# Seven half-block products in the last gated up stage, second homes for the weight sums, and other places for the conditioning turns

## The chip, the core and the metric

One core of a Trainium2 chip runs the whole program. The metric is device time in microseconds (us), as the median of several executions. Profiles come from one execution each.

## What is computed

Two transformer-like blocks for 256 tokens and 1024 features, in fp32. What bears on the change is the last feed-forward part, `conv_ffn` of the second block (there are two of them, one per layer), and the conditioning:

```python
def conv_ffn(h, w_up, conv_w, conv_b, w_down):
    up = h @ w_up                                   # 1024 -> 2 x 2816
    up = lax.conv_general_dilated(up, conv_w[:, None, :], window_strides=(1,), padding=[(CONV_W - 1, 0)],
        dimension_numbers=('NWC', 'WIO', 'NWC'), feature_group_count=2 * D_FF_2) + conv_b     # CONV_W = 3
    val, gate = jnp.split(up, 2, axis=-1)
    return (jax.nn.silu(gate) * val) @ w_down       # 2816 -> 1024

cond = jax.nn.silu(c)
for i in range(DEPTH):
    mod = cond @ ada_w[i] + ada_b[i]                # 1024 -> 6144, for one row
```

The first block has `swiglu` in that place: `(silu(g) * u) @ w_down` without the convolution.

## The kernel before, in words

Activations lie feature-major: a tile is 128 features by 256 tokens. The program is one fixed list of instructions per engine, and semaphores order the engines. `STAGES` names the stages; `up0`, `up1`, `up2`, `up3` are the four gated up products with 44 weight tiles each, that is 22 pairs (gate tile and value tile), and `down0` to `down3` follow them. Both `up0` and `up1` belong to `swiglu`, `up2` and `up3` to `conv_ffn`.

**The ring (SyncE).** All weights come through four ring slots of 512 KB (`ring`, L428). Slot s is reloaded once TensorE has used slot s-4 and, where VectorE reads it too, once the sums are made. One in-order queue issues them. In the same queue stand 96 conditioning loads (`ada_in`, L437), each right behind the slot that `ADA_SLOTS` names. A conditioning load waits on `ada_used` until its home was read by VectorE. There are four homes for the first `N_WIDE` loads and two from then on. While the queue waits for that, no ring slot behind it is issued.

**Conditioning turns (VectorE).** `ada(n)` does n multiply-accumulates over 1024 columns (L2000 for the first of a column of blocks, L2002 else). Where they stand in VectorE's list is written into each stage: `adas_with` in `residual`, `ADA_TWICE` in `up1` (those pairs take two turns), `k >= 4` in `od_xb`, and so on.

**Plain pairs.** `up` (L703) multiplies a weight tile of 1024 x 128 with the tokens: eight matmuls of 256 columns, sixteen records in the trace since each shows as two. `conv_ffn` on ScalarE (L1371) then makes the first tap with the bias for both tiles (L1380) and the SiLU of the gate tile (L1385). On VectorE (L2271) come two more taps per tile (L2291, L2294), and the gate product (L2299). After products 8 and 16 `sum_mids` makes three sums of middle tiles for the down stage (L1794 to L1797).

**Pairs as seven products.** `quick_pair` (L677) computes a pair from half blocks: four of the seven products use sums of weights (`sum_pair`, L2178, four instructions over 512 columns), four use sums of tokens (`sum_tokens`, once per stage). Every product is four matmuls of 128 columns, eight records. Three parts pass through ScalarE, which copies the running sum out of the bank four times (`keep_part`, L1367). VectorE puts them together in `combine_pair` (L2187, L2190). In `up0` all pairs from 2 on go this way. Products 3, 5 and 7 add to the bank that the copies read, so TensorE waits there for `parts_kept`:

```python
pe.wait_ge(pair_sums, 4 * q + 2)
pe.wait_ge(parts_kept, 4 * q + 1)
added_product(chain, s2, t2).then_inc(pair_steps, 1)
```

**Down stages.** `down` (L611) has the same seven-product scheme in chunks; `sum_weights` (L1784) makes four sums per chunk into four homes in `probs_t` and `pair`. Each sum of chunk n waits for TensorE's use of the same sum of chunk n-1 (`weight_sums_used`).

## Time and profile before

| | |
|---|---|
| median of 3 runs | 1678.43 us (1678.21 to 1679.16) |
| the profiled execution | 1679.56 us, its span 1677.8 us |
| mean granted TensorE clock | 0.996 of full speed |
| TensorE busy | 1633.3 us, 97% of the span |
| VectorE busy | 1003.7 us, 60% |
| ScalarE busy | 353.7 us, 21% |
| GpSimd busy | 73.2 us, 4% |
| chain that ended last | TensorE 88%, VectorE 8%, DMA 2% |
| HBM read | 286.68 MB, 171 GB/s over the span |

The chain that ended last is followed back from the last instruction, at each step to what released it. A row of the timeline tells start, duration, engine, line, operation and tiles, and in brackets how long the engine was idle before it and what ended that. "PEclk" is the clock granted to TensorE as a share of full speed. The stages around the change stand at these times of the span: `up0` 238 to 374 us, `od_xb` 443 to 478, `up1` 682 to 839, `up3` 1451 to 1602, `down3` 1602 to 1672.

### The profile page before, as it was taken

To read this page: it belongs to the slowest core of one execution; us is meant where nothing else is said; L and a number is where in the kernel's file an instruction comes from. 1 tells how busy PE (TensorE), PEld (TensorE's weight loads), DVE (VectorE), ACT (ScalarE), POOL (GpSimd) and SP (SyncE) were. 2 spreads that over 40 slices of the span, in tenths; PEclk is the share of its full clock that TensorE was granted. 3 is DMA by queue.
4 is the path that set the end of the run, shared out by engine and by line. 5 is a ranking of instruction groups with operands and counts; after the bars stand their busy time and mean duration, and the time that the engine had idled before them with its cause. 6 is when DMAs were issued, how large, how long until landed. Compare 5 with 4: busy or idle time off the path is not lost.

```text
span 1677.8 us, 27211 instructions
## 1 busy us (share of the span) xinstructions
PE 1633.3 (97%) x10888; PEld 1428.4 (85%) x10888; DVE 1003.7 (60%) x2086; ACT 353.7 (21%) x825; POOL 73.2 (4%) x86
## 2 busy tenths in 40 slices
PE   7999999999989999999999999999999999999998
PEld 6758889999978867788899786688889998888898
DVE  6554668888655334586767577556645683434455
ACT  3241212220151102100001322422213131222200
POOL 0000000000000000195000000000000000000000
PEclk9999999999999999999999999999999999999999
...
GB/s 226 141 145 193 179 217 251 245 223 227 189 161 157 193 319 138 237 238 275 213 169 170 90 118 109 76 149 153 150 139 164 176 3 113 140 152 153 154 169 189
DMA packets 79901, 289.50 MB, mean 173 GB/s; under 512 B 8992, under 2 KB 10016, under 8 KB 79264
## 3 DMA queue, kind: packets, MB, share of 16 engines
...
q8 instruction: 87, 1.43, 0.4%
q14 instruction: 38, 0.31, 0.1%
HBM read 286.68 MB, written 1.05 MB: 171 GB/s over the span
## 4 chain that ended last, share of the span: by engine, by line
PE 88%; DVE 8%; DMA 2%; issue 1%; ACT 1%; SPq 0%; DVEq 0%; ACTq 0%
PE acc L480 46%; PE acc L611 16%; PE acc L669 4%; PE acc L571 4%; PE acc L1134 3%; PE acc L535 2%; PE acc L556 1%; DVE big L2178 1%; DMA ring<-stream 1%; PE acc L490 1%; PE acc L1113 1%; PE score L1099 1%; PE acc L751 1%; DVE bT L2002 1%; PE score L775 1%
## 5 line engine op out<-in xcount | busy, mean ns | idle before, releaser
L480 PE MATMUL acc<-H,ring 128*128 128x256 f32 x2864 | 631.1, 381 | 12.3 <-DMA ring<-stream 8.3
L480 PEld LDWEIGHTS acc<-H,ring 128*128 128x128 f32 x2864 | 544.1, 191 | 95.0 <-DMA ring<-stream 9.7
L480 PE MATMUL acc<-big,ring 128*128 128x256 f32 x880 | 192.2, 379 | 0.9 <-PE acc L480 0.9
L480 PEld LDWEIGHTS acc<-big,ring 128*128 128x128 f32 x880 | 166.8, 190 | 24.8 <-issue 2.3
L2291 DVE SCALAR_TENSOR_TENSOR pair<-acc,cols,pair 128x255 f32<-128x255 f32 x84 | 40.5, 483 | 114.9 <-ACT pair L1380 110.7
L2002 DVE SCALAR_TENSOR_TENSOR bT<-bT,cond 128x1024 f32<-128x1024 f32 x64 | 83.3, 1302 | 39.5 <-DMA bT<-ada_in 34.1
L1784 DVE TENSOR_TENSOR probs_t<-ring 128x512 f32<-128x512 f32 (+1 forms) x96 | 62.1, 647 | 58.5 <-PE acc L611 52.7
L611 PE MATMUL acc<-FFN,ring 128*128 128x128 f32 x760 | 93.6, 275 | 0.0
L611 PEld LDWEIGHTS acc<-FFN,ring 128*128 128x128 f32 x760 | 89.1, 192 | 0.6 <-issue 0.4
L1380 ACT ACTIVATE pair<-acc,cols 128x256 f32<-128x256 f32 x84 | 47.1, 564 | 164.5 <-PE acc L480 164.5
L1212 ACT ACTIVATE SQ<-X 128x256 f32<-128x256 f32 x56 | 23.4, 417 | 181.3 <-DVE X L1760 107.4
L535 PE MATMUL acc<-FFN,ring 128*128 128x256 f32 (+1 forms) x224 | 52.6, 388 | 8.4 <-DMA ring<-stream 8.4
L571 PE MATMUL acc<-ring,big 128*128 128x512 f32 x128 | 56.2, 593 | 1.6 <-DVE big L2402 1.6
L669 PE MATMUL acc<-big 128*128 128x128 f32 x480 | 56.9, 275 | 0.0
L1134 PE MATMUL acc<-MEM,ring 128*128 128x256 f32 x256 | 56.3, 381 | 0.1
L535 PEld LDWEIGHTS acc<-FFN,ring 128*128 128x128 f32 x224 | 43.5, 195 | 14.7 <-issue 8.4
L669 PEld LDWEIGHTS acc<-big 128*128 128x128 f32 x480 | 55.2, 192 | 0.0
L1134 PEld LDWEIGHTS acc<-MEM,ring 128*128 128x128 f32 x256 | 48.3, 190 | 7.2 <-ACT MEM L1606 0.5
L1643 POOL TENSOR_SCALAR chunk_tab<-cols,small 128x64 f32<-128x64 f32 x32 | 19.4, 651 | 706.7 <-DVEq L2064 706.7
L571 PEld LDWEIGHTS acc<-ring,big 128*128 128x128 f32 x128 | 24.2, 190 | 29.6 <-issue 27.3
L611 PE MATMUL acc<-FFN,probs_t 128*128 128x128 f32 x352 | 47.1, 275 | 0.0
L1760 DVE TENSOR_TENSOR X<-acc,X 128x256 f32<-128x256 f32 x32 | 13.6, 425 | 53.9 <-PE acc L480 47.5
...
## 6 DMA issues: line engine op xcount, KB each, us to landing
ring<-stream SPq DMA_DIRECT2D x440, 512.0 KB, 3.6
bT<-ada_in SPq DMA_DIRECT2D x76, 512.0 KB, 5.0
big<-ada_in SPq DMA_DIRECT2D x20, 512.0 KB, 4.8
...
```

Of the source, the lines that this page charges most:

```text
L480: mm = nc.tensor.matmul(dst, w[:, k * cols_per:(k + 1) * cols_per], r, start=first and n == 0, stop=last and n == len(src) - 1)
L535: mm = nc.tensor.matmul(acc[t % 4][:, 0:width], w[:, k * P:(k + 1) * P], src(k, width), start=k == 0, stop=k == KD - 1)
L571: mm = nc.tensor.matmul(acc[(t + b) % 4][:, :], src[:, k * S + b * P:k * S + b * P + P], w[:, k % 2 * 512:(k % 2 + 1) * 512], start=k == 0 ...
L611: mm = nc.tensor.matmul(dst, w[:, k * P:(k + 1) * P], x[k], start=first and k == 0, stop=last and k == len(x) - 1)
L669: mm = nc.tensor.matmul(dst, w[:, k * P:(k + 1) * P], x[k], start=first and k == 0, stop=k == len(x) - 1, skip_group_check=True)
L1134: mm = nc.tensor.matmul(acc[(TILE0["glu"] + k) % 4][:, 0:S], w[:, i * P:(i + 1) * P], at(MEM, i), start=n == 0, stop=n == KD - 1)
L1212: nc.scalar.activation(at(SQ, k), at(src, k), ACT.Square).then_inc(norm_squares, 1)
L1380: nc.scalar.activation(at(pair, 2 * (k % 2) + e), at(FFN, 10 + e) if k == 0 else acc[(TILE0[name] + 2 * k + e) % 4][:, 0:S], ACT.Identity, ...
L1643: ins = g.tensor_scalar(r[:, st * CHUNKS:(st + 1) * CHUNKS], time, turns_hi[:, st:st + 1], None, ALU.mult)
L1784: v.tensor_tensor(dst, x, y, op).then_inc(weight_sums, 1)
L2002: own(v.scalar_tensor_tensor(sums, row, cond[:, k:k + 1], sums, ALU.mult, ALU.add))
L2291: own(v.scalar_tensor_tensor(pair[:, z + 1:z + S], b[:, 0:S - 1], col("fconv_w", c + (3 * layer + 1) * 44), pair[:, z + 1:z + S], ALU.mult ...
```

## The change

1. **`up3`.** Pairs 3 to 20 without 11 and 19, sixteen of 22, go through `quick_pair`. `conv_ffn(1)` becomes `quick_conv_ffn(1)` on ScalarE and on VectorE. Of a plain pair VectorE makes the taps at once (`taps(k - 1)` ahead of the sums for pair k+1); of a seven-product pair behind the gate product of pair k-2 (`late_taps`). `quick_out` grows to two whole tiles, and ScalarE copies the second half of the gate tile there (L1422 of the changed kernel). `up2` stays plain.
2. **Homes of the weight sums.** In `down0` and `down3` they lie in `quick_weights`, two homes taken in turn, so sums for chunk n wait for the uses of chunk n-2. The sums of the first two chunks are issued within the up stage.
3. **Conditioning.** `xo0` takes six turns instead of four, `od_xb` two instead of four (in iterations 5 and 6) with loads behind its slots 0 and 1 alone. In `up0` the 20 turns stand in iterations 0, 1 (two), and 2 to 20 without 9 and 17. In `up1` the pairs with two turns are 11 to 15 and 17, where they were 0, 3, 5, 8, 9 and 10. Four homes serve 44 loads instead of 42.

The core of the diff:

```diff
-ADA_TWICE = (0, 3, 5, 8, 9, 10)
+ADA_TWICE = (11, 12, 13, 14, 15, 17)
+ADA_UP0 = (0, 1, 1) + tuple(k for k in range(2, 21) if k not in (9, 17))
 ADA_SLOTS = [
-    ("ev_out", range(0, 8, 2)), ("xq0", (1, 2, 3, 4, 5, 6, 7, 7)), ("xo0", range(0, 8, 2)),
-    ("up0", range(2, 42, 2)), ("down0", (0, 2, 4, 8, 10, 14)),
-    ("od_xb", (0, 1, 6, 7)),
+    ("ev_out", range(0, 8, 2)), ("xq0", (1, 2, 3, 4, 5, 6, 7, 7)), ("xo0", (0, 1, 2, 4, 5, 6)),
+    ("up0", [2 * k + e for e, k in zip((0, 0, 1) + (0,) * 17, ADA_UP0)]), ("down0", (0, 2, 4, 8, 10, 14)),
+    ("od_xb", (0, 1)),
     ("xq1", (0, 1)), ("xk1", range(8)), ("xv1", range(8)), ("xo1", range(0, 8, 2)),
     ("up1", [2 * k + e for k in range(22) for e in range(2 if k in ADA_TWICE else 1)]),
 ]
 ADA_AFTER = [SLOT0[_name] + i for _name, _at in ADA_SLOTS for i in _at]
 N_ADA = len(ADA_AFTER)
 assert N_ADA == 96 and ADA_AFTER == sorted(ADA_AFTER)
-N_WIDE = 42
+N_WIDE = 44
...
-QUICK = [("up0", 2, 22)]
...
+QUICK = {"up0": range(2, 22), "up3": [k for k in range(3, 21) if k not in (11, 19)]}
+QUICK_AT, QUICK_SLOT = {}, {}
+for _name, _js in QUICK.items():
+    for _j in _js:
+        QUICK_SLOT[SLOT0[_name] + 2 * _j] = QUICK_SLOT[SLOT0[_name] + 2 * _j + 1] = QUICK_AT[_name, _j] = len(QUICK_AT)
...
+QUICK_LAST = {f"down{n[-1]}": max(q for (m, _), q in QUICK_AT.items() if m == n) for n in QUICK}
...
-        summed_weights = [probs_t[:, 0:512], probs_t[:, 512:1024], pair[:, 0:512], pair[:, 512:1024]]
+        def summed_weights(name, n):
+            if name in QUICK_LAST:
+                return quick_weights(QUICK_LAST[name] + 1 + n)
+            homes = (probs_t, 0), (probs_t, 512), (pair, 0), (pair, 512)
+            return [x[:, lo:lo + 512] for x, lo in homes]
...
-            return late[:, 1024 + 384 * (q % 2):1024 + 384 * (q % 2) + 384]
+            return late[:, 1024 + 512 * (q % 2):1024 + 512 * (q % 2) + 512]
...
-                if j == 2:
-                    pe.wait_ge(token_sums, 1)
+                if j == QUICK[name][0]:
+                    pe.wait_ge(token_sums, list(QUICK).index(name) + 1)
...
-                for k in range(2, 2 * quick_from(name)):
+                for k in range(2, 44):
+                    if (name, k // 2) in QUICK_AT:
+                        if k % 2 == 0:
+                            quick_pair(name, k // 2, H)
+                        continue
                     w = slot_in(name, k)
                     bank_free(TILE0[name] + k)
                     product(acc[(TILE0[name] + k) % 4][:, 0:S], w, [at(H, i) for i in range(KD)],
                             fresh=fresh if k == 2 else None).then_inc(slot_used, 1)
                     if between:
                         between(k)
-                for j in range(quick_from(name), 22):
-                    quick_pair(name, j, H)
...
+            def quick_conv_ffn(name, layer):
+
+                i = layer + 2
+                begin(name)
+
+                def first_tap(k):
+                    act.wait_ge(ffn_mid, k + (22 * i + 1))
+                    if (name, k) in QUICK_AT:
+                        act.wait_ge(pair_out, QUICK_AT[name, k] + 1)
...
+                        elif (name, k) in QUICK_AT:
+                            src = at(quick_out(QUICK_AT[name, k]), e)
+                        else:
+                            act.wait_ge(slot_used, RING + SLOT0[name] + 1 + k * 2 + e)
+                            src = acc[(TILE0[name] + 2 * k + e) % 4][:, 0:S]
+                        nc.scalar.activation(at(pair, 2 * (k % 2) + e), src, ACT.Identity, bias=col("fconv_b", c + 44 * layer),
+                                             scale=col("fconv_w", c + (3 * layer + 2) * 44)).then_inc(conv_first, 1)
+
+                def gate(k):
+                    act.wait_ge(taps_out, k + 1)
+                    nc.scalar.activation(at(pair, 2 * (k % 2)), at(pair, 2 * (k % 2)), ACT.Silu).then_inc(silu_done, 1)
+
+                for k in range(1, 24):
+                    quick = (name, k) in QUICK_AT
+                    if (name, k - 1) in QUICK_AT:
+                        q = QUICK_AT[name, k - 1]
+                        if quick:
+                            keep_parts(name, k, range(3))
+                        act.wait_ge(pair_steps, 5 * q + 5)
+                        act.wait_ge(taps_out, k - 1)
+                        own(nc.scalar.activation(quick_out(q)[:, HALF:S], acc[(TILE0[name] + 2 * k - 2) % 4][:, P:2 * P],
+                                                 ACT.Copy))
+                        act.sem_inc(acc_free, 1)
+                        if quick:
+                            keep_parts(name, k, (3,))
+                        gate(k - 2)
+                        first_tap(k - 1)
+                    elif k < 22:
+                        first_tap(k - 1)
+                        if quick:
+                            keep_parts(name, k, range(2))
+                        if k >= 2:
+                            gate(k - 2)
+                        if quick:
+                            keep_parts(name, k, (2, 3))
+                    else:
+                        gate(k - 2)
+                        if k < 23:
+                            first_tap(k - 1)
...
-                    if n:
-                        dve.wait_ge(weight_sums_used, sum_uses(name, n - 1, e))
+                    if n < 2 and name in QUICK_LAST:
+                        dve.wait_ge(pair_steps, 5 * (QUICK_LAST[name] + n))
+                    elif n:
+                        dve.wait_ge(weight_sums_used, sum_uses(name, n - (2 if name in QUICK_LAST else 1), e))
...
-                        if 3 * j + c + 1 < 12:
-                            sum_weights(name, 3 * j + c + 1)
+                        n = 3 * j + c + (2 if name in QUICK_LAST else 1)
+                        if n < 12:
+                            sum_weights(name, n)
...
-                residual(f"xo{layer}", adas_with=4, next_gain=lambda k: col("ffn_norm", 8 * layer + k),
+                residual(f"xo{layer}", adas_with=4 if layer else 6, next_gain=lambda k: col("ffn_norm", 8 * layer + k),
...
-            def combine_pair(name, j):
-
-                q, t = QUICK0[name] + j, TILE0[name] + 2 * j
+            def combine_pair(name, j, tiles_apart):
+
+                q, t = QUICK_AT[name, j], TILE0[name] + 2 * j
+                first, last = (halves(out_of[:, 0:2 * S])[:, 0:4:2, :], out_of[:, 3 * P:4 * P]) if tiles_apart else \
+                    (halves(out_of[:, 0:2 * P]), out_of[:, 2 * P:3 * P])
-                own(v.tensor_tensor(out_of[:, 0:2 * P], parts[:, 0:2 * P], acc[(t + 1) % 4][:, 0:2 * P], ALU.add))
+                own(v.tensor_tensor(first, halves(parts[:, 0:2 * P]), halves(acc[(t + 1) % 4][:, 0:2 * P]), ALU.add))
-                own(v.tensor_tensor(out_of[:, 2 * P:3 * P], parts[:, 3 * P:4 * P], parts[:, 2 * P:3 * P], ALU.add))
+                own(v.tensor_tensor(last, parts[:, 3 * P:4 * P], parts[:, 2 * P:3 * P], ALU.add))
...
-                for k in range(first, 22):
+                for k in range(2, 22):
                     if k < 21:
                         sum_pair(name, k + 1)
-                    if k > first:
+                    if k > 2:
                         gated_tile(k - 1)
-                    if k < 21:
-                        ada(1)
-                    combine_pair(name, k)
+                    ada(ADA_UP0.count(k))
+                    combine_pair(name, k, False)
+                sum_weights(f"down{layer}", 0)
                 gated_tile(21)
+                sum_weights(f"down{layer}", 1)
...
+            def quick_conv_ffn(layer):
+
+                name, i = f"up{layer + 2}", layer + 2
+                inverse_rms(rstd[:])
+                lead_norm(gained_in_ffn, rstd[:], lambda k: mod_col(layer, 3, k))
+                begin(name)
+
+                def taps(k):
+                    for e in range(2):
+                        c = k + (22 if e == 0 else 0)
+                        quick = (name, k) in QUICK_AT
+                        b = at(FFN, 10 + e) if k == 0 else at(quick_out(QUICK_AT[name, k]), e) if quick else \
+                            acc[(TILE0[name] + 2 * k + e) % 4]
+                        z = (2 * (k % 2) + e) * S
+                        dve.wait_ge(conv_first, k * 2 + (8 + 44 * layer + e + 1))
+                        own(v.scalar_tensor_tensor(pair[:, z + 1:z + S], b[:, 0:S - 1], col("fconv_w", c + (3 * layer + 1) * 44),
+                                                   pair[:, z + 1:z + S], ALU.mult, ALU.add))
+                        own(v.scalar_tensor_tensor(pair[:, z + 2:z + S], b[:, 0:S - 2], col("fconv_w", c + 3 * layer * 44),
+                                                   pair[:, z + 2:z + S], ALU.mult, ALU.add))
+                        if not quick and k:
+                            dve.sem_inc(acc_free, 1)
+                    dve.sem_inc(taps_out, 1)
+
+                def gated_tile(k):
+                    dve.wait_ge(silu_done, k + (44 + 8 + 22 + 1))
+                    own(v.tensor_tensor(at(FFN, k), at(pair, 2 * (k % 2)), at(pair, 2 * (k % 2) + 1), ALU.mult))
+                    dve.sem_inc(ffn_mid, 1)
+                    if k in (8, 16):
+                        sum_mids(i, k // 8 - 1)
+
+                for e in range(2):
+                    shifted_lead_tile(name, e, at(FFN, 10 + e), rstd[:])
+                    dve.sem_inc(acc_free, 1)
+                    dve.sem_inc(lead_out, 1)
+                for k in range(1, 22):
+                    late_taps = (name, k - 1) in QUICK_AT
+                    if not late_taps:
+                        taps(k - 1)
+                    if k == 1:
+                        sum_tokens(H)
+                    if k < 21 and (name, k + 1) in QUICK_AT:
+                        sum_pair(name, k + 1)
+                    if k == 20:
+                        sum_weights(f"down{i}", 0)
+                    if k >= 2:
+                        gated_tile(k - 2)
+                    if late_taps:
+                        taps(k - 1)
+                    if (name, k) in QUICK_AT:
+                        combine_pair(name, k, True)
+                sum_weights(f"down{i}", 1)
+                gated_tile(20)
+                taps(21)
+                gated_tile(21)
+                sum_mids(i, 2)
+                paired_residual(f"down{i}", lambda k: mod_col(layer, 5, k))
...
-                if k >= 4:
+                if k in (5, 6):
                     ada(1)
```

**SyncE's queue around `od_xb`.** `ring<-stream` are the weight slots, `bT<-ada_in` conditioning loads. The last slots of `down0` to the first of `xq1`, before:

```order
L428 DMA ring<-stream 128x1024 [waits weight_sums,slot_used] x2
L428 DMA ring<-stream 128x1024 [waits slot_used] x3
L437 DMA bT<-ada_in 128x1024 [waits ada_used]
L428 DMA ring<-stream 128x1024 [waits slot_used]
L437 DMA bT<-ada_in 128x1024 [waits ada_used]
L428 DMA ring<-stream 128x1024 [waits slot_used] x21
```

and in the changed kernel:

```order
L435 DMA bT<-ada_in 128x1024 [waits ada_used]
L426 DMA ring<-stream 128x1024 [waits weight_sums,slot_used]
L435 DMA bT<-ada_in 128x1024 [waits ada_used]
L426 DMA ring<-stream 128x1024 [waits weight_sums,slot_used] x2
L426 DMA ring<-stream 128x1024 [waits slot_used] x25
L435 DMA bT<-ada_in 128x1024 [waits ada_used]
L426 DMA ring<-stream 128x1024 [waits slot_used]
```

The two conditioning loads among the slots of `od_xb` (between x3 and x21) are gone; from the loads at the start of `od_xb` the slots run on to `xq1` without one.

**VectorE, one round in `up3`.** Before, a plain pair (taps from `acc`, a bank of PSUM, and the gate product):

```order
L2291 SCALAR_TENSOR_TENSOR pair<-acc,cols,pair 128x255
L2294 SCALAR_TENSOR_TENSOR pair<-acc,cols,pair 128x254
L2291 SCALAR_TENSOR_TENSOR pair<-acc,cols,pair 128x255
L2294 SCALAR_TENSOR_TENSOR pair<-acc,cols,pair 128x254
L2299 TENSOR_TENSOR FFN<-pair 128x256
```

Now, a pair of seven products (taps of the pair before from `late`, combination, sums of weights, gate product of two pairs before):

```order
L2387 SCALAR_TENSOR_TENSOR pair<-late,cols,pair 128x255
L2389 SCALAR_TENSOR_TENSOR pair<-late,cols,pair 128x254
L2387 SCALAR_TENSOR_TENSOR pair<-late,cols,pair 128x255
L2389 SCALAR_TENSOR_TENSOR pair<-late,cols,pair 128x254
L2247 TENSOR_TENSOR late<-late,acc 128x2x128
L2250 TENSOR_TENSOR late<-late 128x128
L2236 TENSOR_TENSOR big<-ring 128x512
L2236 TENSOR_TENSOR big<-big,ring 128x512
L2236 TENSOR_TENSOR big<-ring 128x512
L2236 TENSOR_TENSOR big<-ring,big 128x512
L2397 TENSOR_TENSOR FFN<-pair 128x256
```

Six instructions were added to the five, and the taps moved behind the gate product of the pair before them.

**ScalarE at the plain pair 11 and the pair of seven products behind it, in the changed kernel** (L1422 is the copy of pair 10, L1412 the gate, L1407 first taps, L1367 kept parts):

```order
L1422 ACTIVATE late<-acc 128x128 [waits taps_out,pair_steps]
L1412 ACTIVATE pair<-pair 128x256 [waits act_own,taps_out]
L1407 ACTIVATE pair<-late,cols 128x256 [waits pair_out,ffn_mid]
L1407 ACTIVATE pair<-late,cols 128x256
L1407 ACTIVATE pair<-acc,cols 128x256 [waits slot_used,ffn_mid]
L1407 ACTIVATE pair<-acc,cols 128x256 [waits slot_used]
L1367 ACTIVATE late<-acc 128x128 [waits pair_steps,pair_out]
L1367 ACTIVATE late<-acc 128x128 [waits pair_steps]
L1412 ACTIVATE pair<-pair 128x256 [waits taps_out]
L1367 ACTIVATE late<-acc 128x128 [waits pair_steps] x2
L1367 ACTIVATE late<-acc 128x128 [waits pair_steps,pair_out]
```

The first taps of the plain pair (from `acc`) stand ahead of all four kept parts of pair 12, and wait on `ffn_mid`, the gate product of pair 9. Between two pairs of seven products three kept parts stand ahead of the gate and the first taps.

## Rows read from the trace of the kernel before

**Rows 1.** the page's part 1: busy us (share of the span) xinstructions
```profile
PE 1633.3 (97%) x10888; PEld 1428.4 (85%) x10888; DVE 1003.7 (60%) x2086; ACT 353.7 (21%) x825; POOL 73.2 (4%) x86
```

**Rows 2.** timeline around `od_xb`: start us, us, engine, line, operation
```profile
466.20 1.29 DVE L2002 SCALAR_TENSOR_TENSOR bT<-bT,cond 128x1024 f32<-128x1024 f32 x1
467.57 0.33 SPq L437 DMA_DIRECT2D bT<-ada_in  x1
...
472.49 5.41 PE L480 MATMUL acc<-H,ring 128*128 128x256 f32 x16 [4.29 <-DMA ring<-stream]
...
477.74 3.62 PE L480 MATMUL acc<-big,ring 128*128 128x256 f32 x16
```

**Rows 3.** timeline of `up1`: SyncE's conditioning load, then TensorE
```profile
689.82 0.33 SPq L437 DMA_DIRECT2D bT<-ada_in  x1
...
694.62 64.11 PE L480 MATMUL acc<-H,ring 128*128 128x256 f32 x288 [3.63 <-DMA ring<-stream]
759.10 79.69 PE L480 MATMUL acc<-H,ring 128*128 128x256 f32 x368 [0.37 <-DMA ring<-stream]
```

**Rows 4.** stretches: PE, PEld, DVE, ACT, POOL busy, PEclk, DMA share, GB/s
```profile
472.40:476.00 3.60, 3.51 (x9) 2.79 (x10) 1.27 (x1) 0.00 (x0) 0.00 (x0) 0.53 0.95 369
694.60:698.00 3.40, 3.38 (x8) 2.76 (x9) 2.77 (x16) 0.00 (x0) 0.00 (x0) 0.51 0.95 373
1339.00:1341.00 2.00, 1.60 (x4) 1.32 (x5) 0.31 (x2) 1.08 (x1) 0.00 (x0) 0.65 0.05 8
```

**Rows 5.** timeline of `up0`, TensorE: last products of pairs
```profile
287.96 1.06 PE L669 MATMUL acc<-H,big 128*128 128x128 f32 x8
...
294.21 1.06 PE L669 MATMUL acc<-H,big 128*128 128x128 f32 x8
...
301.92 1.13 PE L669 MATMUL acc<-H,big 128*128 128x128 f32 x8 [1.29 <-ACT late L1367]
...
354.23 1.13 PE L669 MATMUL acc<-H,big 128*128 128x128 f32 x8 [2.04 <-ACT late L1367]
```

**Rows 6.** timeline of `up0`, VectorE: iteration 9
```profile
292.88 0.69 DVE L2178 TENSOR_TENSOR big<-ring 128x512 f32<-128x512 f32 x1 [0.25 <-DVE late L2190]
...
295.78 0.43 DVE L2197 TENSOR_TENSOR FFN<-pair,late 128x256 f32<-128x256 f32 x1
296.36 0.69 DVE L1794 TENSOR_TENSOR probs<-FFN 128x512 f32<-128x512 f32 x1
...
299.38 0.75 DVE L2000 TENSOR_SCALAR bT<-bT,cond 128x1024 f32<-128x1024 f32 x1
300.35 0.42 DVE L2187 TENSOR_TENSOR late<-late,acc 128x256 f32<-128x256 f32 x1 [0.22 <-DVE bT L2000]
...
301.46 0.69 DVE L2178 TENSOR_TENSOR big<-ring 128x512 f32<-128x512 f32 x1 [0.25 <-DVE late L2190]
```

**Rows 7.** timeline of `up3`: TensorE's plain tiles; VectorE's taps reading FFN
```profile
1459.26 142.72 PE L480 MATMUL acc<-H,ring 128*128 128x256 f32 x660 [0.32 <-DVE H L1747]
...
1460.93 0.48 DVE L2291 SCALAR_TENSOR_TENSOR pair<-FFN,cols,pair 128x255 f32<-128x255 f32 x1 [0.81 <-ACT pair L1380]
1461.45 0.48 DVE L2294 SCALAR_TENSOR_TENSOR pair<-FFN,cols,pair 128x254 f32<-128x254 f32 x1
```

**Rows 8.** stretch of `up1`'s iteration 16, columns as in rows 4
```profile
797.45:804.36 6.91, 6.91 (x34) 6.08 (x33) 5.86 (x9) 0.38 (x1) 0.00 (x0) 1.00 0.70 237
```

**Rows 9.** the page's parts 5 and 6: taps, first taps, ring loads
```profile
L2291 DVE SCALAR_TENSOR_TENSOR pair<-acc,cols,pair 128x255 f32<-128x255 f32 x84 | 40.5, 483 | 114.9 <-ACT pair L1380 110.7
...
L1380 ACT ACTIVATE pair<-acc,cols 128x256 f32<-128x256 f32 x84 | 47.1, 564 | 164.5 <-PE acc L480 164.5
...
ring<-stream SPq DMA_DIRECT2D x440, 512.0 KB, 3.6
```

**Rows 10.** timeline of `up0`, ScalarE: one kept part
```profile
304.04 0.28 ACT L1367 ACTIVATE late<-acc 128x128 f32<-128x128 f32 x1 [0.68 <-PE acc L669]
```

**Rows 11.** timeline of TensorE between `down2` and `s5`: a longer wait
```profile
1339.40 0.99 PE L516 MATMUL stat<-SQ,ones 128*128 128x256 f32 x2 [2.76 <-DVEq L1738]
```

75 lines of the change are left out of this document (37 added, 38 removed).

## The prediction

> **What bounds the kernel now.** I read the page's shares first: TensorE is busy 97% of the span [rows 1], so time is saved only where it gets less work or waits less. Next came the timeline around its longest waits. The first is in `od_xb`: TensorE idles 4.29 us for a ring slot [rows 2]. The cause stands in the same rows. A conditioning turn of VectorE ends at 467.49, SyncE issues the conditioning load that waited for it at 467.57, and only behind it may the queue issue the slot that TensorE needs. The second is the same pattern in `up1`: the conditioning load at 689.82, a wait of 3.63 us, then one of 0.37 [rows 3]. Both long waits are paid twice, because the granted clock behind them is 0.53 and 0.51 of full speed (its lower level, 1.2 of 2.4 GHz) [rows 4]. The sixteen records behind the first take from 472.49 to 477.74, 5.25 us. At full speed a record takes 79.69 / 368 = 0.2165 us [rows 3], so 3.46 were due: 1.79 lost. The 288 records behind the second take 64.11 where 62.37 were due: 1.74 lost.
>
> In `up0`, whose pairs already are seven products, pairs follow each other every 294.21 - 287.96 = 6.25 us, and two waits of 1.29 and 2.04 us for ScalarE's kept parts stand out [rows 5]. They come from VectorE, which has its 3.0 us of middle sums (296.36 to 299.38) on top of a pair's work in those two iterations [rows 6]. In `up3` a plain pair costs 32 records of 142.72 / 660: 6.92 us [rows 7].
>
> The sum is made for the profiled execution, 1679.56 us (a span of 1677.8 and 1.76 around it), 1.13 above the median of 1678.43.
>
> **1. `od_xb`, conditioning moved away.** Slots 6 and 7 no longer carry conditioning loads; two go to `xo0`, where a tile of TensorE (16 records, 3.46 us) leaves VectorE time for an addition, a gain, a square and a turn, some 2.6 us. TensorE's 4.29 and the 1.79 of slow clock go: -6.1. Late next are the convolution's taps for the gates; they end before the gates' third product, so I cost them at nothing. The two turns that stay, in iterations 5 and 6, are covered by the same tiles.
>
> **2. `up1`, double turns moved from pairs 0, 3, 5, 8, 9, 10 to 11 to 15 and 17.** 3.63 + 1.74 + 0.37 = 5.7 go. Against that, VectorE is busy 5.86 of 6.91 us in iteration 16 already [rows 8], and 14 and 15 are alike. One more turn (1.29 [rows 2], 1.43 with its signal) puts each of the two about 0.9 late. Behind the middle sums of iteration 16, VectorE stands 5.0 us behind TensorE's pair: 1.8, less 0.6 of slack that iteration 16 has, 0.2 for the signal, 0.58 for the gate product and 3.0 for the middle sums [rows 6]. The conditioning load of pair 18 waits for that turn, and behind it in SyncE's queue is slot 37. It is issued 6.8 us after pair 16 and lands 3.6 later [rows 9], at 10.4; TensorE wants it at 10.35. The cost lies between nothing and the whole of today's wait with its slow clock, 5.4. I take 0.3, since the sum lands on the edge: -5.4.
>
> **3. `up0`, no turn in iterations 9 and 17.** A first turn of a column takes 300.35 - 299.38 = 0.97 us [rows 6], and VectorE is what ends last there. Each of the two waits shrinks by 0.97: -1.9. The two turns land in iterations 0 and 1. There the two sums for pair 2 still come some 0.7 us before product 3 asks for them: nothing, at most 0.5.
>
> **4. `up3`, sixteen pairs as seven products.** TensorE's part is 16 x (6.92 - 6.25) = -10.7. VectorE now has, per such pair: four weight sums 295.78 - 292.88 = 2.90; the gate product 0.58; four taps at the pitch 0.52 [rows 7] and a signal, 2.2; the combination 301.46 - 300.35 = 1.11 [rows 6]. That is 6.8 us against TensorE's 6.25: VectorE is the bound and drifts 0.54 behind per pair. The order excerpts show that no other work can be dropped from the round.
>
> Where the drift bites, taking the seven products as 0.89 us each:
> - *Start.* The lead tiles, token sums, taps of tile pairs 0 and 1, sums of pair 3 and gate product 0 end at about 1472.7. ScalarE may take the first taps of pair 2 only then (two at 0.56 [rows 9]) and keeps the first part behind them (0.28 [rows 10]). Product 3 of pair 3, due at 1472.4, starts at 1474.25: +1.85.
> - *Pairs 4 to 10.* ScalarE's gate of pair k-2 stands behind its fourth kept part, which follows product 5, at 4.5 us. So VectorE's combination ends 3.0 us into the next pair and drifts to 5.7. There the copy and fourth part come too late for product 7: +0.05, later +0.25.
> - *Pairs 12 and 20, behind the plain ones.* ScalarE's order puts the plain pair's first taps ahead of the kept parts, and they need gate product k-3, which VectorE makes behind the sums of pair k. That is 2.9 us into the pair. Two first taps and a kept part later it is 4.5; product 3 was due at 1.8: +2.7 each.
>
> The waits add up to 7.6, so -3.1 is left. For each term bounds exist: none of the waits (-10.7), or VectorE's whole round exposed (rival 5). A round estimated 0.1 us wrong moves this by 1.5.
>
> The Trainium skill, "VectorE: DVE Perf Modes", section on the TRN2 errata, gives VectorE 62 cycles at 0.96 GHz more from PSUM than from SBUF, an estimate of 0.065 us saved on each tap now that the taps read SBUF. By that the sum would be about 3.9 us better. The rows disagree: a first tap reading FFN takes 0.48 [rows 7], and the mean of the PSUM ones is 483 ns [rows 9]; I go by them.
>
> **5. `down0` and `down3`.** Two homes for the weight sums let VectorE run ahead of TensorE. The first sums of `down3` are issued before gate product 18 and the second before 20, so the start of the stage no longer waits for chunk 0. But the middle sums come later by the drift, and I find about as much wait at chunk 2: nothing.
>
> Sum: 6.1 + 5.4 + 1.9 + 3.1 = 16.5. The profiled execution would be 1663.1 and the median **1661.9**.
>
> **The rivals.**
> 1. *VectorE's round hides after all* (the waits of step 4 do not appear; up3 gives 10.7): 1661.9 - 7.6 = 1654.3. For it: no resource forbids it at the start of each run of pairs. Against: 6.8 is added from measured pitches. 0.13.
> 2. *Taps from SBUF are quicker than from PSUM.* If they took the 0.42 of the two-tensor addition [rows 6] instead of 0.48, the round would be 6.56, 0.24 less over some 15 rounds: 3.6, so 1658.3. This is the mechanism of the errata section above. Against it the 0.48 of the FFN row. 0.05.
> 3. *The clock falls behind the two waits of 2.7 us.* A wait of 2.76 us elsewhere in this trace [rows 11] is followed by a granted clock of 0.65 [rows 4]; whether one of 2.7 does the same is open. Two losses like that of `up1`, 1.74 each: 1665.4. 0.14.
> 4. *The conditioning waits come back elsewhere*, in `up1` behind the double turns or at the start of `up0`: one more loss of 5.4: 1667.3. 0.10.
> 5. *Slower.* ScalarE and VectorE take turns in `up3` instead of overlapping: gate waits for taps, gate product for gate, first taps for gate product. If two first taps, a copy, a kept part and the gate (1.13 + 0.28 + 0.28 + 0.42 = 2.1) stand in series with the 6.8, a pair costs 8.9 and the stage 16 x 2.0 = 32 more: 1678.4 - 13.4 + 32 = 1697. It decides from 7.76 us per pair, where the stage has lost the 13.4 of the other steps, that is from 1.0 us of ScalarE in series. Against it: ScalarE's order lets first taps of pair k-1 run while VectorE makes sums. 0.04.
> 6. *The seven products bring nothing and a moved wait stays*: 1673 to 1678. 0.04.
>
> **The numbers.** The forecast's own chance is 0.50, its own range 1658.5 to 1665.5. Around 1653.5 rival 1 ends, and 1669 takes in rival 4; outside lie rivals 5 and 6 and a part of the others, under 2 in 10. A difference under 0.2% (3.4 us) can't be told from none. Rivals 1 to 4 and most of 6 are faster by more: 0.94. Within: 0.02. Slower: 0.04.
>
> **What would show it.** Right: no wait for the ring at `od_xb` or at the start of `up1` and full clock there; `up0`'s two waits near 0.3 and 1.1; in `up3` VectorE nearly without idle time, its rounds at 6.8 us, TensorE waiting about 2.7 us at product 3 of pairs 12 and 20 and 1.9 at pair 3, stage time some 139.5. Wrong: rounds of 6.5 or less, granted clock under 1.00 behind those waits, a new wait for the ring near pair 18 of `up1`, or `up3` no shorter than 142.

## The result and the profile after

The changed kernel takes 1670.34 us (median of 4 runs, 1669.69 to 1671.13); the kernel before took 1678.8 beside it. The ratio is 0.9945, 95% interval [0.9931, 0.9959]: faster by 8.5 us. I had forecast 16.5 (1661.9), and 1670.34 lies above the range of 1658.5 to 1665.5. The profiled execution is one of 1669.97 us, with a span of 1668.1 for 1677.8 before.

The page's part 1 of the changed kernel, which answers to [rows 1]:

```profile
PE 1622.9 (97%) x11272; PEld 1431.3 (86%) x11272; DVE 1060.6 (64%) x2186; ACT 370.4 (22%) x905; POOL 70.0 (4%) x86
```

TensorE's busy time fell by 10.4 us and VectorE's rose by 57. The share of TensorE stayed at 97%. Where the time went shows when the program is cut at TensorE's records. Each row runs from the first product of the stage to the first product of what follows; "norm sums" are the records `stat<-SQ,ones` that start the norm behind a down stage or within an up stage. The numbers are starting times from the two timelines, subtracted; `down3` runs to the end of its last product. `gates` is the stage behind `od_xb`, and `up3` starts with its two lead tiles, the two around its norm sums. There is one trace of each kernel.

| stretch | before | after | gain | forecast |
|---|---|---|---|---|
| `up0`, pairs 2 to 21 | 129.15 | 126.40 | 2.75 | 1.9 |
| `down0` to its norm sums | 74.23 | 78.75 | -4.52 | 0 |
| norm sums to `gates` | 29.56 | 23.31 | 6.25 | 6.1 |
| `up1` from its norm sums | 157.41 | 153.14 | 4.27 | 5.4 |
| `up3` | 154.52 | 153.76 | 0.76 | 3.1 |
| `down3`, to its end | 70.11 | 70.76 | -0.65 | 0 |
| sum | | | 8.86 | 16.5 |

The last 1.0 us lies in other stretches: 0.62 ahead of `up0`, where TensorE's first wait for a load is 7.60 us for 8.39, and 0.40 between `up1` and `up3`, which the change doesn't touch. Of the 7.6 us that the forecast was too high, 4.5 were lost in `down0`, 2.3 in `up3`, 1.1 in `up1` and 0.65 in `down3`; `up0` and `od_xb` gave 1.0 more.

**`od_xb` and `up1`**, TensorE's timeline and, between, SyncE's. Columns as in [rows 2]:

```profile
455.38 17.43 PE L478 MATMUL acc<-H,ring 128*128 128x256 f32 x80
472.64 3.65 PE L478 MATMUL acc<-big,ring 128*128 128x256 f32 x16
...
799.95 0.33 SPq L435 DMA_DIRECT2D bT<-ada_in  x1
800.32 0.91 SPq L426 DMA_DIRECT2D ring<-stream  x2
...
804.99 24.44 PE L478 MATMUL acc<-H,ring 128*128 128x256 f32 x112 [1.68 <-DMA ring<-stream]
```

The 4.29 us wait of [rows 2] and the slow records behind it are gone: 80 records in 17.43 us. In `up1` the waits of [rows 3] are gone too, and one new one stands at 804.99. It has the same pattern: the ring's load at 800.32 stands behind the conditioning load at 799.95, and that one waited for VectorE's turn.

**`down0`**, TensorE's waits in its timeline, then VectorE's timeline between them:

```profile
394.40 2.02 PE L609 MATMUL acc<-FFN,ring 128*128 128x128 f32 x16 [0.21 <-DMA ring<-stream]
403.08 0.94 PE L609 MATMUL acc<-H,big 128*128 128x128 f32 x6 [0.85 <-DVE big L1841]
413.37 2.02 PE L609 MATMUL acc<-FFN,ring 128*128 128x128 f32 x16 [0.42 <-DMA ring<-stream]
423.50 0.94 PE L609 MATMUL acc<-H,big 128*128 128x128 f32 x6 [2.30 <-DVE big L1841]
...
406.55 1.28 DVE L2060 SCALAR_TENSOR_TENSOR bT<-bT,cond 128x1024 f32<-128x1024 f32 x1
413.31 1.42 DVE L1841 TENSOR_TENSOR big<-ring 128x512 f32<-128x512 f32 x2 [5.48 <-DMA ring<-stream]
...
416.21 1.28 DVE L2060 SCALAR_TENSOR_TENSOR bT<-big,cond,bT 128x1024 f32<-128x1024 f32 x1
417.65 0.42 DVE L1866 TENSOR_TENSOR late<-late,acc 128x256 f32<-128x256 f32 x1
...
421.70 1.15 DVE L1841 TENSOR_TENSOR big<-ring 128x384 f32<-128x384 f32 x2
```

Read it from below. The 2.30 us wait at 423.50 is for sums that VectorE begins only at 421.70. Before them it made the combination of the tile pair (from 417.65), before that a conditioning turn, and before that the sums of a chunk two ahead, for which it stood 5.48 us idle at an empty ring slot. The tile pair's last product ended before 406.6, so the combination could have been made in that idle time, but it comes later in VectorE's order. The ring holds four slots, two chunks; the chunk two ahead can only be loaded once the present one has been used.

**`up3`**, TensorE's timeline at pairs 3, 12 and 20:

```profile
1464.32 1.91 PE L667 MATMUL acc<-big 128*128 128x128 f32 x15 [1.54 <-ACT late L1367]
1524.30 2.92 PE L667 MATMUL acc<-big 128*128 128x128 f32 x24 [2.14 <-ACT late L1367]
1578.16 4.54 PE L667 MATMUL acc<-big 128*128 128x128 f32 x24 [2.14 <-ACT late L1367]
```

Stretches behind the last two (columns as in [rows 4]):

```profile
1524.00:1528.00 4.00, 3.70 (x33) 3.73 (x34) 3.21 (x8) 1.29 (x5) 0.00 (x0) 1.00 0.33 119
1578.00:1582.00 4.00, 3.84 (x20) 3.87 (x21) 2.82 (x6) 0.87 (x4) 0.00 (x0) 0.59 0.33 121
```

The same 24 records (three products) take 2.92 us after the one wait of 2.14 us and 4.54 after the other, where the granted clock is 0.59. Around pair 12, first VectorE, then ScalarE:

```profile
1519.55 0.69 DVE L2236 TENSOR_TENSOR big<-ring 128x512 f32<-128x512 f32 x1 [0.25 <-DVE late L2250]
...
1522.45 0.42 DVE L2397 TENSOR_TENSOR FFN<-pair 128x256 f32<-128x256 f32 x1
...
1522.97 1.02 ACT L1407 ACTIVATE pair<-acc,cols 128x256 f32<-128x256 f32 x2 [2.42 <-DVEq L2398]
1523.88 0.27 ACT L1367 ACTIVATE late<-acc 128x128 f32<-128x128 f32 x1
```

The gate product (1522.45) stands behind the 2.9 us of sums that begin at 1519.55. ScalarE waits 2.42 us for it with its first taps, and the kept part that TensorE needs at 1524.30 comes behind those. VectorE's round is what was forecast. Its timeline, the combinations of three quick pairs (pairs of seven products) in a row:

```profile
1491.07 0.42 DVE L2247 TENSOR_TENSOR late<-late,acc 128x256 f32<-128x256 f32 x1 [0.21 <-DVE pair L2389]
1497.91 0.42 DVE L2247 TENSOR_TENSOR late<-late,acc 128x256 f32<-128x256 f32 x1 [0.21 <-DVE pair L2389]
1504.74 0.42 DVE L2247 TENSOR_TENSOR late<-late,acc 128x256 f32<-128x256 f32 x1 [0.21 <-DVE pair L2389]
```

A round takes 6.83 to 6.84 us against TensorE's 6.25. The taps in the view of groups of this stage, each shape apart:

```profile
L2387 DVE SCALAR_TENSOR_TENSOR pair<-late,cols,pair 128x255 f32<-128x255 f32 x30 | 14.5, 483 | 2.7
L2387 DVE SCALAR_TENSOR_TENSOR pair<-acc,cols,pair 128x255 f32<-128x255 f32 x8 | 3.9, 483 | 1.7 <-ACT pair L1407 0.7
```

A tap takes 483 ns from SBUF (`late`) and 483 from PSUM (`acc`).

### The profile page after: what moved, and what is told of

Same layout as the page of the kernel before. It is cut to its first block, busy times and chain, and to the rows that moved or that the text cites. A ratio compares the mean times of both kernels' runs of the same rounds, so it can differ in the third digit from the quotient of the medians.

```text
span 1668.1 us, 28348 instructions
## 1 busy us (share of the span) xinstructions
PE 1622.9 (97%) x11272; PEld 1431.3 (86%) x11272; DVE 1060.6 (64%) x2186; ACT 370.4 (22%) x905; POOL 70.0 (4%) x86
## 4 chain that ended last, share of the span: by engine, by line
PE 80%; DVE 13%; DMA 2%; issue 2%; ACT 2%; SPq 0%; DVEq 0%; ACTq 0%
PE acc L478 36%; PE acc L609 14%; PE acc L667 8%; PE acc L569 4%; PE acc L1134 3%; DVE big L2236 3%; PE acc L533 2%; DMA ring<-stream 2%; PE acc L554 1%; PE acc L488 1%; PE acc L1113 1%; PE score L1099 1%; DVE pair L2387 1%; DVE pair L2389 1%; PE acc L751 1%
## 5 line engine op out<-in xcount | busy, mean ns | idle before, releaser
L478 PE MATMUL acc<-H,ring 128*128 128x256 f32 x2352 | 517.2, 380 | 5.7 <-DMA ring<-stream 1.7
L478 PEld LDWEIGHTS acc<-H,ring 128*128 128x128 f32 x2352 | 444.5, 190 | 73.2 <-issue 7.9
L667 PE MATMUL acc<-big 128*128 128x128 f32 x864 | 104.2, 278 | 5.8 <-ACT late L1367 5.8
L667 PEld LDWEIGHTS acc<-big 128*128 128x128 f32 x864 | 101.0, 195 | 6.3 <-issue 6.3
L667 PE MATMUL acc<-H,ring 128*128 128x128 f32 x576 | 70.2, 275 | 0.0
L667 PEld LDWEIGHTS acc<-H,ring 128*128 128x128 f32 x576 | 67.5, 192 | 0.2
L1367 ACT ACTIVATE late<-acc 128x128 f32<-128x128 f32 x144 | 39.8, 276 | 119.0 <-PE acc L667 118.5
L2236 DVE TENSOR_TENSOR big<-ring 128x512 f32<-128x512 f32 x72 | 49.8, 692 | 12.7 <-DVE late L2250 5.0
L1841 DVE TENSOR_TENSOR big<-ring 128x512 f32<-128x512 f32 (+1 forms) x48 | 31.1, 647 | 39.7 <-DMA ring<-stream 29.6
L1841 DVE TENSOR_TENSOR probs_t<-ring 128x512 f32<-128x512 f32 (+1 forms) x48 | 31.1, 647 | 30.1 <-PE acc L609 22.7
```

The lines of the kernel that those rows point to most:

```text
L478: mm = nc.tensor.matmul(dst, w[:, k * cols_per:(k + 1) * cols_per], r, start=first and n == 0, stop=last and n == len(src) - 1)
L667: mm = nc.tensor.matmul(dst, w[:, k * P:(k + 1) * P], x[k], start=first and k == 0, stop=k == len(x) - 1, skip_group_check=True)
L1367: nc.scalar.activation(kept(q)[:, n * P:(n + 1) * P], acc[(t + n // 2 % 2 * (n < 3)) % 4][:, P:2 * P], ACT.Copy)\
L1841: v.tensor_tensor(dst, x, y, op).then_inc(weight_sums, 1)
L2236: v.tensor_tensor(dst, x, y, op).then_inc(pair_sums, 1)
```

## The experiments

Three losses were to be explained: 4.5 us in `down0`, the waits in `up3`, and the wait in `up1`. My theories: sums issued two chunks ahead hold VectorE at the ring (A); a gate product behind long sums holds ScalarE (C); double turns too late in `up1` hold SyncE (E). The rivals: the moved conditioning costs what `down0` lost (B), and VectorE's long round sets the pace wherever the waits stand (D). Ratios are to the kernel before on the same chip; the changed kernel's is 0.9945.

### e1: the moved turns alone

The kernel before with part 3 of the change, nothing of parts 1 and 2:

```diff
-ADA_TWICE = (0, 3, 5, 8, 9, 10)
+ADA_TWICE = (11, 12, 13, 14, 15, 17)
+ADA_UP0 = (0, 1, 1) + tuple(k for k in range(2, 21) if k not in (9, 17))
...
-    ("od_xb", (0, 1, 6, 7)),
+    ("od_xb", (0, 1)),
...
-                if k >= 4:
+                if k in (5, 6):
                     ada(1)
```

> The kernel before with the moved conditioning turns alone: last up stage plain, every weight sum in one home. Theory A (the moved turns pay as the trace of the changed kernel shows them: od_xb 6.2, up1 9.36 less 5.1, 4.3, up0 about 3.5, and down0 keeps its 68.9 us because the loss there belongs to the two homes): 14.0 us faster than before, 1664.8, and so 5.5 faster than the changed kernel. Theory B (the 4.7 us that down0 lost come from the moved turns and their loads): 9.3 us faster than before, 1669.5, with down0 at 73.6 us.

Measured: 1666.6 us, ratio 0.9922 [0.9908, 0.9936]. Its interval overlaps the changed kernel's by 0.0005, but its slowest execution (1668.18, on another chip) is below the changed kernel's fastest (1669.69). From `down0` to its norm sums 74.77 us: theory A. `up0` has 125.41 us, so its part is 3.7. The gain is 13.1 and not 14.0. One loss is in `up1`. Its wait in TensorE's timeline:

```profile
801.13 26.13 PE L481 MATMUL acc<-H,ring 128*128 128x256 f32 x112 [2.04 <-DMA ring<-stream]
```

The stretch behind it, columns as in [rows 4]:

```profile
801.00:806.00 5.00, 4.87 (x15) 3.96 (x16) 4.29 (x7) 0.00 (x0) 0.00 (x0) 0.66 1.03 419
```

The 112 records take 26.13 us here and 24.44 in the changed kernel. Against that, this trace has 1.9 us of luck where nothing was changed: from the end of `up1` to `up3` it takes 606.69 us for 608.57 before, mostly because the clock did not fall behind a wait of 2.76 us there (last section). Parts 1 and 2 of the change together cost about 4.6 us (13.1 less 8.5) of what part 3 brings.

### e2: `down0` with one home, sums one chunk ahead

```diff
-QUICK_LAST = {f"down{n[-1]}": max(q for (m, _), q in QUICK_AT.items() if m == n) for n in QUICK}
+QUICK_LAST = {f"down{n[-1]}": max(q for (m, _), q in QUICK_AT.items() if m == n) for n in QUICK if n != "up0"}
...
-                sum_weights(f"down{layer}", 0)
                 gated_tile(21)
-                sum_weights(f"down{layer}", 1)
+                sum_weights(f"down{layer}", 0)
```

> The changed kernel, with down0's weight sums back in one home and one chunk ahead. Theory A (two chunks ahead puts sums that wait for the ring ahead of turns, combination and due sums): down0 back from 73.6 to about 68.9 us, the time 4.7 lower, 1665.6. Theory B (the moved conditioning costs the 4.7): no change, 1670.3.

Measured: 1666.03 us, ratio 0.9920 [0.9907, 0.9934]; `down0` to its norm sums 75.33 us, 1.08 of it one wait for the ring. Theory A holds, theory B falls. `up3` and `down3` are those of the changed kernel here, and the time is e1's to 0.6 us: as made, the sixteen pairs bring nothing. The traces agree: from `up3`'s lead tiles to the last product the kernel before takes 224.63 us, e1 224.62, the changed kernel 224.52.

### e3: `down0` with two homes, sums one chunk ahead

```diff
                 gated_tile(21)
-                sum_weights(f"down{layer}", 1)
...
-                        n = 3 * j + c + (2 if name in QUICK_LAST else 1)
+                        n = 3 * j + c + (2 if name == "down3" else 1)
```

> The changed kernel, down0 still with two homes, but each chunk's sums issued one chunk ahead, not two. Theory A1 (the order on VectorE is the cost, not the homes): down0 at 68.9 to 69.3 us, 1665.6 to 1666.0. Theory A2 (the homes themselves cost, by where they lie or what they wait for): stays near 73.6 and 1670.3. Theory B: 1670.3.

Measured: 1667.34 us, ratio 0.9922 [0.9909, 0.9934]; `down0` to its norm sums 74.69 us, 4.06 less than in the changed kernel. The homes cost nothing, the order does (A1). The median is 3.0 us lower and not 4.1. The profiled execution (1667.85) loses 2.0 in `up1`, where its wait of 1.99 us is followed by slow records (26.13 us for the 112); another execution took 1664.53. VectorE's timeline in the place that was shown above, one tile pair earlier: the combination now stands ahead of the wait.

```profile
388.81 0.75 DVE L2058 TENSOR_SCALAR bT<-bT,cond 128x1024 f32<-128x1024 f32 x1
389.71 0.42 DVE L1866 TENSOR_TENSOR late<-late,acc 128x256 f32<-128x256 f32 x1
...
394.43 1.42 DVE L1841 TENSOR_TENSOR big<-ring 128x512 f32<-128x512 f32 x2 [1.50 <-issue]
```

### e4: the gate product ahead of the sums

```diff
+                    if k in (2, 11, 19):
+                        gated_tile(k - 2)
                     if k < 21 and (name, k + 1) in QUICK_AT:
                         sum_pair(name, k + 1)
...
-                    if k >= 2:
+                    if k >= 2 and k not in (2, 11, 19):
                         gated_tile(k - 2)
```

> The changed kernel; in up3, where the pair two ahead of a quick pair's sums is due (rounds 2, 11, 19), VectorE forms the gated tile before the 2.9 us of sums and not behind them. Theory C (ScalarE's first tap of the plain pair waits for that tile, and keeps the first parts of pairs 3, 12 and 20 late behind itself: 1.54, 2.14 and 2.14 us, and 1.7 of slow clock after the last): these waits go, some come back as VectorE is late by its rounds of 6.86 us; 5 us lower, 1665.3 (range 1663.0 to 1667.5), clock 1.00 at pair 20. Theory D (VectorE's rounds of 6.86 us against TensorE's 6.25 set the pace, wherever the wait stands): the waits move to other pairs and at most 1.7 us, the clock, is saved: 1668.6 or more.

Measured: 1666.79 us, ratio 0.9921 [0.9909, 0.9933]. `up3` takes 149.71 us, 4.05 less, of which 1.6 is the slow clock behind pair 20's wait; forecast 5, and theory D would have allowed 1.7. VectorE, ScalarE and TensorE around pair 12:

```profile
1518.67 0.42 DVE L2397 TENSOR_TENSOR FFN<-pair 128x256 f32<-128x256 f32 x1
1519.35 0.69 DVE L2236 TENSOR_TENSOR big<-ring 128x512 f32<-128x512 f32 x1 [0.25 <-DVE FFN L2397]
...
1520.59 0.28 ACT L1367 ACTIVATE late<-acc 128x128 f32<-128x128 f32 x1
...
1525.02 1.16 PE L667 MATMUL acc<-big,ring 128*128 128x128 f32 x8 [0.96 <-ACT late L1367]
```

The first kept part now ends at 1520.87, ahead of TensorE. But 0.96 us come back at a later product of the same pair, as they do at pair 20 (0.95), and five waits of 0.34 to 0.36 stand at other pairs: 3.6 us in all. I read this as VectorE's lag, theory D's part of the truth; e8 tries it.

### e5: turns ahead of sums in `down0`

```diff
+                        if (j, c) in adas_at:
+                            ada(1)
                         n = 3 * j + c + (2 if name in QUICK_LAST else 1)
                         if n < 12:
                             sum_weights(name, n)
-                        if (j, c) in adas_at:
-                            ada(1)
```

> The changed kernel; in down0 the conditioning turn of a chunk stands ahead of the sums issued two chunks ahead, not behind them. Theory A3 (SyncE's queue is the link: a conditioning load waits for a turn, the turn stands behind sums that wait for a ring slot, and that slot's load stands behind the conditioning load): at least the 0.21 and 0.42 us behind the ring and most of the 0.85 and 2.30 us behind sums go; down0 4 us shorter, near 1666.3. Theory A4 (two chunks ahead is too far in itself, since the sums keep VectorE from the combination and the next due sums): at least 2 us stay, 1668.3 or more.

Measured: 1668.35 us, ratio 0.9929 [0.9917, 0.9941]; `down0` to its norm sums 77.57 us, 1.2 less than in the changed kernel. So the turn behind the sums is 1.2 of the 4.1 us; more than 2 stay, as A4 said. VectorE still stands 4.81 and 4.92 us at the ring. Theory A3 had it that the waits for the ring go. They grew, from 0.21 and 0.42 us to 0.37 and 1.40, while those for sums shrank from 0.85 and 2.30 to one of 0.86. TensorE's timeline:

```profile
413.50 2.02 PE L609 MATMUL acc<-FFN,ring 128*128 128x128 f32 x16 [1.40 <-DMA ring<-stream]
```

### e6: double turns elsewhere in `up1`

```diff
-ADA_TWICE = (11, 12, 13, 14, 15, 17)
+ADA_TWICE = (4, 9, 11, 12, 13, 17)
```

> The changed kernel; up1's double turns at pairs 4, 9, 11, 12, 13, 17 and not at 11 to 15, 17. Theory E (VectorE, 6.1 to 6.3 of 7 us busy from pair 12 on, runs its turns late behind the double ones at 14 and 15 and the middle sums, so SyncE's conditioning load at 799.95 is late and the weight tile behind it too): the 1.68 us at 804.99 goes, 1668.6, and with it the slow clock that followed the same wait in e1 and e3. Theory F (the late slot is the double turn at pair 17): the wait stays, 1670.3. A double turn at pair 4 could instead bring a new ring wait early in the stage, at most 2 us.

Measured: 1668.45 us, ratio 0.9928 [0.9915, 0.9941]. No wait for the ring is left in `up1`. The stage ends at 828.22, the changed kernel's at 829.36, though `down0`'s norm sums came 0.56 us later (behind the wait of 2.31 us in `down0` the clock fell here): 1.7 us, theory E. The double turn at pair 17 stays and is harmless, so theory F falls.

### e7: e3, e4 and e6 together

```diff
-ADA_TWICE = (11, 12, 13, 14, 15, 17)
+ADA_TWICE = (4, 9, 11, 12, 13, 17)
...
-                        n = 3 * j + c + (2 if name in QUICK_LAST else 1)
+                        n = 3 * j + c + (2 if name == "down3" else 1)
...
+                    if k in (2, 11, 19):
+                        gated_tile(k - 2)
```

> Three edits on the changed kernel together: down0's sums one chunk ahead (3.0 us alone by the medians, 4.1 by the stage), gated tile ahead of the sums in up3 (3.5 to 4.1 alone), double turns of e6 (1.7, 3.4 where the clock fell). If they are independent: 1660.5 (1659.5 to 1662). If VectorE's lag is passed from stage to stage: 1663 or more.

Measured: 1659.23 us, ratio 0.9874 [0.9861, 0.9888], just below the range for independent edits; nothing of one is lost by the others. `down0` to its norm sums takes 74.01 us, `up1` 151.60 and `up3` 149.82, where e3 has 74.69, e6 151.41 and e4 149.71.

### e8: three plain pairs inside `up3`

```diff
-QUICK = {"up0": range(2, 22), "up3": [k for k in range(3, 21) if k not in (11, 19)]}
+QUICK = {"up0": range(2, 22), "up3": [k for k in range(3, 21) if k not in (7, 12, 17)]}
```

The gate product ahead of the sums moves with the plain pairs, to rounds 2, 7, 12 and 17.

> e7, and in up3 three plain pairs inside the quick ones (7, 12, 17) in place of two (11, 19): 15 pairs as seven products. Theory G (after e4 the waits left in up3, five of 0.35 us and two of 0.95, are VectorE's lag of 0.61 us a quick round and 2.9 us for each set of middle sums, which a plain pair lets it make good): the third plain pair costs 0.7 us and the 3.6 us of waits go to 1 or less, 2 us below e7. Theory H (those waits come from ScalarE's own queue, not from lag): they stay and e8 is 0.7 us above e7.

Measured: 1658.22 us, ratio 0.9867 [0.9853, 0.9881], 1 us under e7 with an interval that holds e7: by the medians nothing is told. By the trace, `up3` takes 148.66 us for e7's 149.82. Of e4's seven waits one of 0.34 is left, as theory G said, but 1.36 us came at pair 11, whose round has the middle sums, and 1.59 at the start of `down3`. So the waits in sum did not fall to 1 us, and the 2 us that G forecast were not won.

### e9: no conditioning in `down0`

```diff
+ADA_LEFT_OUT = range(38, 44)
...
+                    if a in ADA_LEFT_OUT:
+                        dve.sem_inc(ada_used, 1)
+                        continue
```

> The changed kernel, sums two chunks ahead, with the six conditioning turns of down0 and their six loads left out (six of 96 blocks of the conditioning product are missing). It asks what makes two chunks ahead cost here and nothing in down3. From down0's first product to the sums of the norm behind it: 78.75 us in the changed kernel, 77.57 in e5, 74.69 in e3. Theory A5 (the loads between the ring's loads and the turns keep the ring late; without them two chunks ahead is harmless): 74.2 to 75.0. Theory A6 (two chunks ahead alone keeps VectorE at the ring and the combination behind it): 77 or more.

Measured: 1664.84 us, ratio 0.9911 [0.9895, 0.9926]; six of the 96 blocks are missing from its output. `down0` starts at 369.31 and its norm sums at 443.28, 73.97 us with no wait of TensorE between, where theory A6 had 77 or more. So in `down0` the loss needs both: sums two chunks ahead, and the six conditioning blocks. This run has the first without the second, e3 the second without the first (74.69). VectorE still stands 5.46 us at the ring here, with the combination behind it at 394.78, and TensorE does not wait for it. VectorE's timeline:

```profile
391.77 1.42 DVE L1843 TENSOR_TENSOR big<-ring 128x512 f32<-128x512 f32 x2 [5.46 <-DMA ring<-stream]
```

What about the blocks it is, this run doesn't tell: it leaves out their loads, which stand between the ring's loads in SyncE's queue, and their turns, 0.75 to 1.28 us of VectorE each, together. e5 puts 1.2 us on the place of the turns; the rest is open between the two.

### e10: e1 with the double turns of e6

```diff
-ADA_TWICE = (11, 12, 13, 14, 15, 17)
+ADA_TWICE = (4, 9, 11, 12, 13, 17)
```

> e1 with the double turns of e6: the kernel before with all moved turns and without the change to the last up stage. e1's 1666.6 less the 2.04 us ring wait and the 1.7 us of slow clock behind it: 1663.0. With it, e7 (1659.23) is the seven products' own worth when their order is mended: Theory I, 3.5 to 4 us, as the stage of e7 says (149.8 for 154.5, less 0.2 to 0.6 given back in down3); Theory J: less than 2, if e7's gain is mostly the turns: 1661 or less.

Measured: 1665.03 us, ratio 0.9913 [0.9899, 0.9928], 2 us above theory I's number and 4 above theory J's. The wait at 801 went, and a new one came behind the double turn at pair 9:

```profile
744.58 17.75 PE L481 MATMUL acc<-H,ring 128*128 128x256 f32 x81 [1.56 <-DMA ring<-stream]
```

e6, e7, e8 and e12, with the same table, have no wait there; e11, with the same table too, has 0.64. So this place is an edge; what decides it was not tried. For the seven products the trace answers better than the medians, whose difference to e7 (5.8 us) also holds this wait. From `up3`'s lead tiles to the end e10 takes 224.63 us and e7 220.12. In good order they are worth 4.5 (theory I, a little more).

### e11: plain pairs at 6, 11 and 17, sums of `down3` behind the last combination

```diff
-QUICK = {"up0": range(2, 22), "up3": [k for k in range(3, 21) if k not in (7, 12, 17)]}
+QUICK = {"up0": range(2, 22), "up3": [k for k in range(3, 21) if k not in (6, 11, 17)]}
...
-                        n = 3 * j + c + (2 if name == "down3" else 1)
+                        n = 3 * j + c + 1
...
-                    if k == 20:
-                        sum_weights(f"down{i}", 0)
...
-                sum_weights(f"down{i}", 1)
+                sum_weights(f"down{i}", 0)
                 gated_tile(20)
```

The diff is against e8. The later sums of `down3` come one chunk ahead, not two, and the gate product ahead of the sums moves with the plain pairs.

> e8 with its plain pairs at 6, 11 and 17, and down3's first sums behind the last combination, the later ones one chunk ahead. e8 waited 1.36 us at pair 11 (middle sums in that round), 0.34 at pair 20 and 1.59 at down3's start, where the combination of pair 20 stood behind sums that waited for the ring. If lag and that order are the causes, all three go: 1655.2 (1654.5 to 1656.5). If lag is not the cause the wait moves with the pair: 1656.6.

Measured: 1655.78 us, ratio 0.9860 [0.9845, 0.9875]. TensorE's waits for kept parts in `up3`, from its timeline:

```profile
1517.32 1.16 PE L667 MATMUL acc<-big,ring 128*128 128x128 f32 x8 [0.70 <-ACT late L1367]
1544.05 1.13 PE L667 MATMUL acc<-H,big 128*128 128x128 f32 x8 [0.35 <-ACT late L1367]
1570.65 1.13 PE L667 MATMUL acc<-H,big 128*128 128x128 f32 x8 [0.69 <-ACT late L1367]
```

The 1.59 us at `down3`'s start and the 1.36 are gone. 1.74 remain in `up3`, where I had expected none, and 0.37 in `down3`. The medians can't tell my two numbers apart (1655.2 if lag is the cause, 1656.6 if the wait moves with the pair); that the long wait did not move with the pair speaks for lag. `down3` takes 69.58 us for 70.31 in e8.

### e12: four plain pairs, 6, 10, 14 and 18

```diff
-QUICK = {"up0": range(2, 22), "up3": [k for k in range(3, 21) if k not in (6, 11, 17)]}
+QUICK = {"up0": range(2, 22), "up3": [k for k in range(3, 21) if k not in (6, 10, 14, 18)]}
```

> As e11 with four plain pairs, 6, 10, 14, 18: 14 pairs as seven products. If e11 has no waits left inside up3, this one is 0.7 us slower than it; if e11 still waits over 0.7 us for VectorE, equal or faster.

Measured: 1656.12 us, ratio 0.9863 [0.9846, 0.9879], equal to e11, as expected of a kernel whose waits exceed 0.7 us. `up3` takes 147.32 us for 147.41. So fourteen pairs bring what fifteen do; sixteen, in the order of e7, bring less (149.82). Sixteen with e11's order of `down3`'s sums were not tried. e11 and e12 are faster than the kernel before by 1.4% and than the changed kernel by about 14 us.

## Why the prediction was wrong

**Step 5 failed: "Two homes let VectorE run ahead of TensorE ... nothing".** I asked whether TensorE would wait for sums less often, and did not ask what VectorE itself waits for when it runs ahead. The ring was in the profile: 3.6 us from issue to landing [rows 9], four slots, and chunks of up to 6.25 us. A sum two chunks ahead waits for a load that can't start before the present chunk is used. Whatever stands behind that sum in VectorE's order (a turn, the combination, the next sums) waits with it. The step cost 4.5 us in `down0`; e3 takes back 4.1, and e9 shows that the loss needs the conditioning blocks too. In `down3`, which has none, the step was half right: the wait for chunk 0 went, as said, but the one at chunk 2 is longer. TensorE's timeline, before and after:

```profile
1605.55 1.16 PE L611 MATMUL acc<-probs,probs_t 128*128 128x128 f32 x8 [0.90 <-DVE probs_t L1784]
```

```profile
1606.87 0.91 PE L609 MATMUL acc<-H,big 128*128 128x128 f32 x6 [1.47 <-DVE big L1841]
```

That is 0.57 of the 0.65 us lost there. Two homes let VectorE run ahead only as far as the ring does.

**Step 4 had the mechanism, and a size off.** Right: 6.25 us a pair; 6.84 a round of VectorE for 6.8; waits at pair 3 (1.54 for 1.85), pair 12 (product 3 at 1524.30, due 1.79 behind the pair's start at 1520.21: 2.3 for 2.7) and pair 20. Pairs 3 to 10 took 52.47 us, 2.5 more than 8 x 6.25, where the forecast had 2.2. Too small was pair 20's term: it had 2.7 and came to 4.0, since the clock fell behind its wait (1.6 to 1.7 us), which I held for rival 3. All waits and slow records together are 9.7 us where the step had 7.6. So `up3` gained 0.76 us and not 3.1, and `down3` lost 0.65 of that.

I also took the order of VectorE as given. "No other work can be dropped from the round" was true and beside the point: e4 moved one instruction of 0.42 us ahead of the sums in three rounds, and won 4.

**Step 2** had the mechanism and sized its last term wrongly. Slot 37 (seven tiles from the end of `up1`) came late behind a conditioning load, as reckoned, by 1.68 us in place of 0.3. The loss had been said to lie "on the edge", and the runs show what the edge means. With the same turns in `up1` this wait is 1.16 us in e9, 1.68 in the changed kernel, 1.79 in e2, 1.99 in e3, 2.01 in e4, 2.04 in e1 and 3.18 in e5, with the slow clock behind it in e1, e3 and e5; e10, with other turns, has 1.56 in another place. **Step 1** was right to 0.15 us. **Step 3** was short by 0.85: the two waits shrank from 1.29 to 0.23 and from 2.04 to 0.30 [rows 5], by 2.8 together and not by 0.97 each. Why more than the turn's length went was not tried. In e2, with the same turns, the first wait is 1.02 us, so these waits also differ from trace to trace.

**The rivals.** Rival 1 fell: the round shows. Rival 2 fell: with 483 ns from `late` and 483 ns from `acc` in one stage, the case speaks against the Trainium skill, "VectorE: DVE Perf Modes", section on the TRN2 errata, for this operation. Rival 3 was right in one of its two places. Rival 4 was right in a smaller size, 1.68 for 5.4. Rival 6 (the seven products bring nothing), at 0.04, was what happened in `up3` and `down3`, 0.1 us together; I had given it little, since I saw no mechanism. The time itself stayed below that rival's 1673 to 1678, by what the moved turns brought. Mechanisms for both halves of it were in this text: rival 3, and the round that is longer than TensorE's.

Of the four signs of being wrong that I had named, two were there: a granted clock under 1.00 behind a wait of `up3`, and a new wait for the ring near pair 18 of `up1`.
